# Two-block transformer kernel: second memory value slab moved into the cross attention's steps, query tiles on steps 4, 6, 8 and 10

## The reference, cut to what matters

```python
def cross_attention(xn, memn, w_q, w_kv, w_o):
    b, s, _ = xn.shape
    q = (xn @ w_q).reshape(b, s, XATTN_HEADS, XATTN_HEAD_DIM)
    k, v = jnp.split(memn @ w_kv, 2, axis=-1)
    k = k.reshape(b, -1, XATTN_HEADS, XATTN_HEAD_DIM)
    v = v.reshape(b, -1, XATTN_HEADS, XATTN_HEAD_DIM)
    scores = jnp.einsum('bqhd,bkhd->bhqk', q, k).astype(jnp.float32) * (XATTN_HEAD_DIM ** -0.5)
    p = jax.nn.softmax(scores, axis=-1).astype(v.dtype)
    o = jnp.einsum('bhqk,bkhd->bqhd', p, v).reshape(b, s, D_MODEL)
    return o @ w_o
...
        x = x + token_mixer(rmsnorm_2(x, norm_mix[l]), ...)
        x = x + cross_attention(rmsnorm_2(x, norm_xattn[l]), rmsnorm_2(mem, norm_mem[l]),
                                w_xq[l], w_xkv[l], w_xo[l])
        x = x + squared_relu_mlp(rmsnorm_2(x, norm_mlp[l]), w_up[l], w_down[l])
```

## Time and profile before

| what | value |
|---|---|
| median of three runs | 1886.1 us |
| the profiled execution's own time | 1887.72 us |
| its span in the profile | 1885.9 us |
| TensorE (PE) matmul busy | 1780.3 us, 94% |
| DVE busy | 964.3 us, 51% |
| ACT busy | 665.6 us, 35% |
| share of the chain that ended last: PE | 84% |
| the same: DVE, ACT, issue | 6%, 5%, 2% |
| DMA | 166.26 MB, mean 88 GB/s |

### The profile page before, as it was taken

How to read it: one execution, slowest core, us unless ns; L and a number is a source line. 1 busy time by engine, 2 the same in 40 slices (tenths; PEclk the granted TensorE clock), 3 DMA queues, 4 the chain that set the end, 5 groups by cost and what they waited for, 6 DMA issues and landing times.

```text
span 1885.9 us, 18182 instructions
## 1 busy us (share of the span) xinstructions
PE 1780.3 (94%) x6946; PEld 1246.3 (66%) x6946; DVE 964.3 (51%) x1328; ACT 665.6 (35%) x993; POOL 155.8 (8%) x160
## 2 busy tenths in 40 slices
PE   7999898988899999998999898989998999999997
PEld 1378643355688888886765455446886778888886
DVE  5657555355464424433476676377543254434343
ACT  2531244312343313325442542543543243323132
POOL 0302200014200000003000000023200100000001
PEclk9999999999999999999999999999999999999999
DMA  9324310421213232223131111101521122222331
GB/s 320 113 92 157 112 35 11 152 94 45 91 51 117 79 112 90 89 84 117 45 111 64 70 45 45 48 0 63 184 89 46 45 89 90 89 89 89 113 109 44
DMA packets 98353, 166.26 MB, mean 88 GB/s; under 512 B 3371, under 2 KB 39723, under 8 KB 98092
## 3 DMA queue, kind: packets, MB, share of 16 engines
q1 hardware_dynamic: 94524, 152.63, 23.5%
q0 software_dynamic: 3760, 12.72, 2.1%
HBM read 163.23 MB, written 2.10 MB: 88 GB/s over the span
## 4 chain that ended last, share of the span: by engine, by line
PE 84%; DVE 6%; ACT 5%; issue 2%; DMA 1%; POOL 1%; SPq 0%; DVEq 0%; ACTq 0%; POOLq 0%
PE bank L726 12%; PE bank L727 12%; PE bank L728 12%; PE bank L759 6%; PE bank L760 6%; PE bank L764 5%; PE bank L713 4%; PE bank L939 3%; PE bank L780 3%; PE bank L1107 3%; PE bank L1165 2%; PE bank L969 2%; PE bank L829 1%; PE bank L982 1%; PE bank L909 1%
## 5 line engine op out<-in xcount | busy, mean ns | idle before, releaser
L2650 POOL TENSOR_TENSOR arena<-arena 128x512 f32<-128x512 f32 (+1 forms) x56 | 72.7, 1308 | 985.4 <-ACT arena L1335 981.6
L759 PE MATMUL bank<-xn_hi,weights_hi 128*128 128x512 f32 x320 | 127.4, 398 | 6.2 <-ACT xn_hi L1320 6.2
L760 PE MATMUL bank<-xn_hi,weight_slots_lo 128*128 128x512 f32 x320 | 127.1, 397 | 0.0
L1315 ACT ACTIVATE weights_hi<-weight_slots 128x2048 fp32r<-128x2048 f32 (+2 forms) x46 | 77.0, 1725 | 121.5 <-DMA weight_slots<-in_ffn_w_down 67.1
L1871 ACT ACTIVATE weights_hi<-weight_slots 128x2048 fp32r<-128x2048 f32 x30 | 55.8, 1908 | 162.8 <-DMA weight_slots<-in_w_up 109.1
L713 PE MATMUL bank<-arena,weight_slots 128*128 128x512 f32 x256 | 112.2, 592 | 0.0
L726 PE MATMUL bank<-xn_hi,weights_hi 128*128 128x512 f32 x288 | 112.0, 389 | 0.0
L727 PE MATMUL bank<-xn_lo,weights_hi 128*128 128x512 f32 x288 | 112.0, 389 | 0.0
L728 PE MATMUL bank<-xn_hi,weight_slots_lo 128*128 128x512 f32 x288 | 112.0, 389 | 0.0
L2607 DVE TENSOR_TENSOR weight_slots_lo<-weight_slots,weights_hi 128x2048 fp32r<-128x2048 f32 x30 | 67.4, 2289 | 86.3 <-ACT weights_hi L1871 86.3
L1302 ACT ACTIVATE arena<-bank 128x512 f32<-128x512 f32 (+3 forms) x110 | 54.7, 538 | 139.6 <-PE bank L728 50.6
(11 more groups left out here) (402 smaller groups left out, 3822.8 us busy)
## 6 DMA issues: line engine op xcount, KB each, us to landing
weight_slots<-in_w_in SPq DMA_DIRECT2D x30, 1024.0 KB, 7.2
weight_slots<-in_ffn_w_up SPq DMA_DIRECT2D x22, 1024.0 KB, 7.2
weight_slots<-in_w_mod SPq DMA_DIRECT2D x16, 1024.0 KB, 7.6
weight_slots<-in_w_up SPq DMA_DIRECT2D x16, 1024.0 KB, 6.4
weight_slots<-in_w_down SPq DMA_DIRECT2D x16, 1024.0 KB, 6.4
arena<-in_w_mod POOLq DMA_DIRECT2D x32, 256.0 KB, 3.4
weight_slots<-in_w_out SPq DMA_DIRECT2D x8, 1024.0 KB, 7.4
weight_slots<-in_w_xkv SPq DMA_DIRECT2D x8, 1024.0 KB, 7.5
```

Source lines behind the costliest of these rows:

```text
L759: mm(ps[:, 0:width], wh(k, m), x2[0][:, k, 0:width], start=k == 0, stop=False)
L760: mm(ps[:, 0:width], wl(k, m), x2[0][:, k, 0:width], start=False, stop=False)
L1315: A(high(kind, n)[:, a:b], W[:, s_, a:b], ACT.Copy).then_inc(w_hi, 1)
L2650: G.tensor_tensor(acc, acc, sq[i % 2][:, 0:width], ALU.add).then_inc(sq_added, 1)
```

## The change: what it does

The second value slab's two products leave their place ahead of the queries and go to steps 1 and 2 of the attention (`XV_STEPS`). The query tiles 4 to 7 go from steps 3, 5, 8, 10 to 4, 6, 8, 10. The slabs are loaded in the order xv 0, xq 0, xv 1, xq 1 instead of xv 0, xv 1, xq 0, xq 1. ACT and DVE split xq 0 where they split xv 1 before, xv 1 after the activations' split, and xq 1 inside the steps, at their step 2. The head output waits for its own value slab alone.

```diff
-XQ_STEPS = [3, 5, 8, 10]
+XQ_STEPS = [4, 6, 8, 10]
+XV_STEPS = [1, 2]
...
-    j += [f"xk_{g}" for g in range(4)] + [f"xv_1_{t}" for t in range(2)]
+    j += [f"xk_{g}" for g in range(4)]
     j += [f"xq_{m}" for m in range(4)]
...
+        if n in XV_STEPS:
+            j += [f"xv_1_{XV_STEPS.index(n)}"]
         if n in XQ_STEPS:
...
-    s += [("xk", n, f"xkt_{n}_1") for n in range(2)] + [("xv", n, f"xv_{n}_1") for n in range(2)]
-    s += [("xq", n, f"xq_{4 * n + 3}") for n in range(2)]
+    s += [("xk", n, f"xkt_{n}_1") for n in range(2)]
+    s += [(kind, n, f"xv_{n}_1" if kind == "xv" else f"xq_{4 * n + 3}") for n in range(2) for kind in ("xv", "xq")]
...
             first_products("xq", "xa", (xq_hi, xq_lo))
-            w_xq = split_slab("xq", 1)
             for g in range(4):
                 evicted(pe, f"xk_{g}")
-            for n in range(2):
-                for t in range(2):
-                    evicted(pe, f"xv_{n}_{t}")
+            for t in range(2):
+                evicted(pe, f"xv_0_{t}")
...
+                if n in XV_STEPS:
+                    t_ = XV_STEPS.index(n)
+                    token_product(f"xv_1_{t_}", t_, "mem", hm_hi, hm_lo, split_slab("xv", 1))
                 if n in XQ_STEPS:
                     m = XQ_STEPS.index(n)
+                    if m == 0:
+                        w_xq = split_slab("xq", 1)
                     split_product(f"xq_{4 + m}", w_xq, m, "xa", (xq_hi, xq_lo))
                 if n >= 2:
                     if t == NT - 1:
                         for t in range(NT):
                             evicted(pe, f"xt_{h}_{t}")
+                        for t in range(2):
+                            evicted(pe, f"xv_{h // 2}_{t}")
...
+            split_w("xq", 0)
+            for k in range(4):
+                act.wait_ge(normed, first + k + 1)
+                split_x(xq_hi[:, k, :], xq_in[:, k, :])
+            for t in range(2):
+                values_out(0, t)
+            for k in range(4, KD):
+                act.wait_ge(normed, first + k + 1)
+                split_x(xq_hi[:, k, :], xq_in[:, k, :])
+            for g in range(4):
+                copy(kmem[:, 2 * g:2 * g + 2, :], f"xk_{g}", PS[jobs[f"xk_{g}"] % 8][:].rearrange("p (m t) -> p m t", m=2))
...
-            split_w("xq", 1)
+            split_w("xv", 1)
             for m in range(4):
                 queries_out(m)
...
                 if 2 <= n < XH * NT + 2:
                     probs_out(*divmod(n - 2, NT))
+                if n - 1 in XV_STEPS:
+                    values_out(1, XV_STEPS.index(n - 1))
+                if n == 2:
+                    split_w("xq", 1)
...
             normalise("norm_xa", lambda k: x[:, k, :], lambda k: pc("norm_xattn_2", k), lambda k: xq_in[:, k, :])
+            split_w("xq", 0)
+            for k in range(KD):
+                split_x("xa", k, xq_lo[:, k, :], xq_in[:, k, :], xq_hi[:, k, :])
             split_w("xv", 1)
-            for k in range(4):
-                split_x("xa", k, xq_lo[:, k, :], xq_in[:, k, :], xq_hi[:, k, :])
-            split_w("xq", 0)
-            for k in range(4, KD):
-                split_x("xa", k, xq_lo[:, k, :], xq_in[:, k, :], xq_hi[:, k, :])
-            split_w("xq", 1)
...
                 if n >= NT and n % NT == 2:
                     heads_low(n // NT - 1)
+                if n == 2:
+                    split_w("xq", 1)
```

More of the change, by code:

```diff
@@ L1181, in _ @@
                     norm_sum("norm_xa")
-            for n in range(2):
-                w = split_slab("xv", n)
-                for t in range(2):
[L1185 to L1188, removed]
-                        for t in range(2):
[L1190 to L1194, removed]
+            w = split_slab("xv", 0)
+            for t in range(2):
+                token_product(f"xv_0_{t}", t, "mem", hm_hi, hm_lo, w)
+            for g in range(4):
+                ps = begin(f"xk_{g}")
+                for t in range(2):
+                    evicted(pe, f"xkt_{g // 2}_{t}")
+                for i in range(4):
+                    m, t = 2 * g + i // 2, i % 2
+                    ins = nc.tensor.transpose(ps[:, P * i:P * i + P], xk_rows[:, t, P * m:P * m + P], ident)
+                end(ins)
             first_products("xq", "xa", (xq_hi, xq_lo))
-            w_xq = split_slab("xq", 1)
             for g in range(4):
                 evicted(pe, f"xk_{g}")
-            for n in range(2):
-                for t in range(2):
-                    evicted(pe, f"xv_{n}_{t}")
+            for t in range(2):
+                evicted(pe, f"xv_0_{t}")
             def probs_T(h, t):
@@ L1804, in _, with values_out @@
             first = norms["norm_xa"][0]
[L1805 to L1814, removed]
+            def values_out(n, t):
+                copy(vmem[:, t, 512 * n:512 * n + 512], f"xv_{n}_{t}", PS[jobs[f"xv_{n}_{t}"] % 8][:])
+            split_w("xq", 0)
+            for k in range(4):
+                act.wait_ge(normed, first + k + 1)
+                split_x(xq_hi[:, k, :], xq_in[:, k, :])
+            for t in range(2):
+                values_out(0, t)
+            for k in range(4, KD):
+                act.wait_ge(normed, first + k + 1)
+                split_x(xq_hi[:, k, :], xq_in[:, k, :])
+            for g in range(4):
+                copy(kmem[:, 2 * g:2 * g + 2, :], f"xk_{g}", PS[jobs[f"xk_{g}"] % 8][:].rearrange("p (m t) -> p m t", m=2))
             def queries_out(m):
                 copy(qx[:, m, :], f"xq_{m}", PS[jobs[f"xq_{m}"] % 8][:])
-            split_w("xq", 1)
+            split_w("xv", 1)
             for m in range(4):
```

## The result

The changed kernel takes 1895.54 us, the median of six runs (1892.1 to 1900.85), against 1886.55 us for the kernel before (six runs, 1885.2 to 1893.41). The ratio is 1.0049, with a 95% interval of 1.0032 to 1.0065: slower by 9 us, clear of the 0.2% that count as no change.

What follows compares the result with a forecast made beforehand. TensorE, busy for 94% of the span, was taken to bound the kernel, so only its waits could change. Terms -0.3 + 4.0 + 1.6 + 0.4 = +5.7, with the clock +7.4, gave 1893.5 us, range 1889.8 to 1896.0.

Steps and rivals of the forecast that it cites:

- The sum: Whole kernel: all five terms together, +5.7 us without the clock's fall and +7.4 us with it, median 1893.5 us.
- Term 1: Attention step 2: the moved value products cover the 0.30 us wait there, -0.3 us.
- The sooner start: Ahead of the steps: queries start 10.9 us sooner, near 1373.5, with slab xq 0 split in time; cost nothing.
- Term 2: Ahead of xq_4: TensorE waits for DVE's split of xq 1, queued behind the maximum of tile 3; +4.0 us.
- Terms 3 and 4: New wait ahead of head 0's output, +1.6 us; wait ahead of scores 8 grows from 1.48 to 1.89, +0.4 us.
- Term 5: Behind the 4 us wait: TensorE's clock falls to half rate, +1.7 us from a possible 0 to 2.9.
- The split is in time: Rival at DVE's step 2: xq 1 ready when TensorE asks, +1.7 us, 1887.8 us, no change; chance 0.07.
- Banks: Rival in the steps: four waits hang on banks and could go, 6.8 us, leaving +0.6, 1886.7 us; chance 0.04.
- late landing: Rival at xq 1's load: beyond some 4 us late each further us costs one, 1896.5 at 3 more; chance 0.04.
- the clock stays up: Rival behind the 4 us wait: no fall to half rate, +5.7 us, 1891.8 us; chance 0.30.

Runs made afterwards that it cites:

- the fill: Against the changed kernel, sixteen 128x512 matmuls on xq_hi put ahead of the wait for slab xq 1: 1898.0 us, ratio 1.0045 to the kernel before.
- the query tiles alone: The kernel before with query tiles 4 to 7 at steps 4, 6, 8, 10 and nothing else changed: 1890.06 us, ratio 1.0022.
- the later split: Against the changed kernel, ACT and DVE split xq 1 at step 3 instead of 2: 1899.67 us, ratio 1.0072 to the kernel before.
- query tile 4 at step 5: Against the changed kernel, query tiles at steps 5, 6, 8, 10: 1891.91 us, ratio 1.0039 to the kernel before.
- the value slab alone: Against the kernel before, second value slab moved to steps 1 and 2, xq 1 split at step 1, query tiles kept at 3, 5, 8, 10: 1886.97 us, ratio 1.0007.

## Why the prediction was right, point by point

- **The sum.** +7.4 us was forecast, 1893.5 us; measured were 1895.54, inside the range of 1889.8 to 1896.0 but only 0.5 below its upper end, and +9.0. In the traces, where the rest of the program doesn't scatter in, the attention became 7.7 us longer, 6.0 of waits and 1.6 of clock, against 5.7 and 1.7 forecast.
- **Term 1 (-0.3), the moved products.** The wait at step 2 is gone, as said. But other small waits grew by about as much (four from step 9 on by 0.35 together in the change), so the move came out at nothing and not at a gain.
- **The sooner start.** Queries at 1373.0, scores near 1395, nothing held up. Right.
- **Term 2 (+4.0), the wait for the split of xq 1.** 3.96 measured, ended by DVE as said, with the split begun at 1410.63 where "near 1411" was forecast. Moving the split one step sooner took the wait away, one step later made it 6.79. This step carries the result, and it came from reading DVE's order and not the DMA: ACT's half was done 2 us before DVE began.
- **Terms 3 and 4 (+1.6, +0.4).** 1.62 and 1.89 - 1.48 = 0.41. The shape of a step, which product stands ahead of which wait, gave both lengths from other steps of the same trace.
- **Term 5 (+1.7), the clock.** 7.17 - 5.56 = 1.6 in the place, eight matmuls at half rate. The reason for choosing 1.7 was weak: the prediction took the one wait that follows full work, but the 2.96 us one that left the clock up follows full work too (matmuls 0.23 us apart until 467 in the kernel before). That the fall came is shown; that 1.7 was the right pick between 0 and 2.9 is partly luck. The Trainium skill's warning (TensorE: Matmul & The Clock Gate, "Why this matters for your kernels") held here: the trace shows 0.50 behind the gap, and 1.00 with the gap filled. The 3.08 us gap ahead of the MLP, behind which four of ten traces stayed at 1.00, shows that a gap of about three us need not bring the fall. The fill bought nothing in the median, so the term is right for its place and unsettled for the whole.
- **What was too small.** The range allowed one change of the clock elsewhere, 1.3 us each way. The traces show more of it: 2.9 us at the start of the MLP, more in the steps of the kernels with longer waits. The kernel with the query tiles alone came out 2 us above the sum of its two waits. In the medians of the change the clock's share is about 3 us by the estimate above, where the sum has 1.7. The waits as forecast and that larger share make up the +8 to +9.
- **The rivals.** "The split is in time" gave +1.7, and the kernel in which it is in time measured +2.1. "Banks", "late landing" and "the clock stays up" didn't occur.

## What to carry to other kernels

When a piece of preparation (here a slab's split of 4.5 us) is moved into a pipelined loop, look at what stands directly ahead of it in its own engine's order: behind an instruction that waits for another engine it inherits that wait, however early its data is there. Put it ahead of that instruction, so that it fills the idle time instead of following it.

A product on the busiest engine is worth moving only to a place with a wait. List the waits of a relay by shape and lay the movable products in front of the largest. With the value slab moved and the split in time, the same query tiles gave +2.1 us at steps 4, 6, 8, 10, nothing to tell at 3, 5, 8, 10, and -4.3 at 5, 6, 7, 9.

## What the runs showed of the hardware

The clock's fall isn't tied to one place. Behind the same wait of 3.08 us at the start of the MLP matmuls ran at 1.2 GHz in six of the ten traces (fourteen of them in the kernel before) and none did in the other four. Within the steps it also fell behind shorter waits: behind the 1.89 us ahead of scores 12 the granted clock was 0.50 to 0.53 in five traces (the fill, the later split, query tile 4 at step 5, the query tiles alone, the value slab alone) and stayed 1.00 in both traces of the change and in the one of before. In the trace of the query tiles alone no wait in the steps was longer than 1.9 us, and it fell twice.

In runs of one kernel the time goes with the mean granted clock: for the kernel before, 1885.04 us at 0.981 to 1892.29 at 0.976 on one chip, and 1881.76 at 0.984 to 1892.82 at 0.976 on the other. So a change of 2 us needs many runs, a comparison of runs with the same mean clock, or a length read within the trace.
